# A hybrid decoder layer: the sparse-attention indexer and half of its top-k search interleaved with a reordered input projection, fp32 products in place of hi/lo stacks

## What is computed

```python
s = jnp.einsum('bqhd,bsd->bqhs', qi, ki).astype(jnp.float32)          # 8 indexer heads of 64
score = jnp.einsum('bqhs,bqh->bqs', jax.nn.relu(s), wi) * IDX_SCALE
score = jnp.where(causal[None], score, -jnp.inf)
_, sel = lax.top_k(score, n_sel)                                      # 256 keys of each query
k_sel = gather(k, sel); v_sel = gather(v, sel)
logits = jnp.einsum('bqhd,bqkd->bhqk', q, k_sel) * DSA_HD ** -0.5     # 4 heads, one key head
a = jax.nn.softmax(logits, axis=-1)
return jnp.einsum('bhqk,bqkd->bqhd', a, v_sel)
```

## Time and profile before

| | |
|---|---|
| median of 3 runs | 2062.38 us (2059.34 to 2068.35) |
| span of the profiled execution | 2056.5 us |
| TensorE busy | 1782.8 us (87%), weight loads 1599.2 us |
| DVE busy | 1014.8 us (49%) |
| ACT busy | 629.8 us (31%) |
| POOL busy | 39.9 us (2%) |
| projection | 37 to 297 us |
| values, maps, index stage | 297 to 417 us |
| diff and sdiff items | 417 to about 760 us |
| dsa and sdsa items | about 760 to 947 us |
| output projection, MLP, embedding, last norm | 947 us to the end |

### The profile page before, as it was taken

One profiled execution on the slowest core, in us unless ns is written; L12 is line 12 of the kernel. 1 busy time (PEld: TensorE's weight loads), 2 busy tenths in 40 slices (PEclk: granted clock), 3 DMA queues, 4 the chain that ended last, 5 costly groups with the idle time before them and its releaser, 6 DMA issues.

```text
span 2056.5 us, 26558 instructions
## 1 busy us (share of the span) xinstructions
PE 1782.8 (87%) x9933; PEld 1599.2 (78%) x9933; DVE 1014.8 (49%) x2033; ACT 629.8 (31%) x1083; POOL 39.9 (2%) x43
## 2 busy tenths in 40 slices
PE   3999996847788976998979999999999999998794
PEld 3999983424455665667969999999899899998794
DVE  5113406787778885333344444534443443454643
ACT  3111125555456733443122211121121121113321
POOL 0000000000000002001000000000000000000000
PEclk9999996855566555887989999999999999999897
DMA  3111112111211112113101111111111111120102
GB/s 143 41 51 41 51 53 61 27 41 57 67 42 41 42 41 62 31 32 142 45 27 42 41 52 42 42 42 45 49 41 42 42 42 51 41 67 31 31 31 84
DMA packets 48043, 102.80 MB, mean 50 GB/s; under 512 B 5378, under 2 KB 21762, under 8 KB 47938
## 3 DMA queue, kind: packets, MB, share of 16 engines
q1 hardware_dynamic: 45506, 92.44, 14.4%
q0 software_dynamic: 2432, 8.92, 1.2%
HBM read 93.69 MB, written 7.66 MB: 49 GB/s over the span
## 4 chain that ended last, share of the span: by engine, by line
PE 68%; DVE 13%; issue 9%; ACT 4%; SPq 2%; DMA 2%; POOL 1%; DVEq 0%; POOLq 0%; ACTq 0%
PE ps L213 41%; PE ps L1364 10%; PE ps L533 3%; PE ps L494 2%; PE ps L519 2%; DVE TN L818 2%; PE ps L447 1%; DVE TN L266 1%; DVE Z L971 1%; PE ps L1499 1%; SPq L1101 1%; PE ps L545 1%; PE ps L1185 1%; DMA pages<-in_d_pages 1%; SPq L1102 1%
## 5 line engine op out<-in xcount | busy, mean ns | idle before, releaser
L213 PE MATMUL ps<-xh,wh 128*128 128x352 f32 x1968 | 640.7, 326 | 34.6 <-DVE xl L271 21.6
L213 PE MATMUL ps<-xh,wl 128*128 128x352 f32 x1968 | 638.0, 324 | 0.0
L213 PE MATMUL ps<-xl,wh 128*128 128x352 f32 x1968 | 637.7, 324 | 0.0
L213 PEld LDWEIGHTS ps<-xh,wh 128*128 128x128 f32 x1968 | 372.7, 189 | 40.5 <-issue 26.2
L213 PEld LDWEIGHTS ps<-xh,wl 128*128 128x128 f32 x1968 | 372.7, 189 | 0.0
L213 PEld LDWEIGHTS ps<-xl,wh 128*128 128x128 f32 x1968 | 372.3, 189 | 0.0
L204 ACT ACTIVATE wh<-wr 128x1024 fp32r<-128x1024 f32 x106 | 112.1, 1059 | 849.6 <-PE ps L213 604.8
L208 DVE TENSOR_TENSOR wl<-wr,wh 128x1024 fp32r<-128x1024 f32 x106 | 129.5, 1223 | 431.2 <-ACT wh L204 431.1
L1364 PE MATMUL ps<-ah,wh 128*128 128x352 f32 x528 | 175.3, 332 | 18.0 <-DVE Z L1443 17.9
L1443 DVE TENSOR_TENSOR Z<-Z,ps 128x352 f32<-128x352 f32 x264 | 134.5, 520 | 98.3 <-PE ps L1364 97.8
L1364 PE MATMUL ps<-al,wh 128*128 128x352 f32 x528 | 169.9, 322 | 0.0
(11 more groups left out here) (247 smaller groups left out, 1884.7 us busy)
## 6 DMA issues: line engine op xcount, KB each, us to landing
wr<-in_weights SPq DMA_DIRECT2D x106, 512.0 KB, 3.6
pages<-in_d_pages SPq DMA_DIRECT2D x64, 256.0 KB, 2.9
pages<-in_c_pages SPq DMA_DIRECT2D x64, 96.0 KB, 1.9
Z<-in_xT SPq DMA_DIRECT2D x8, 528.0 KB, 8.7
Z<-in_xT POOLq DMA_DIRECT2D x8, 528.0 KB, 8.1
out_y<-TN SPq DMA_DIRECT2D x8, 528.0 KB, 2.7
arena<-in_c_pages SPq DMA_DIRECT2D x64, 64.0 KB, 1.8
out_d_k<-Z POOLq DMA_DIRECT2D x2, 528.0 KB, 6.5
```

Of the source, the lines that this page charges most:

```text
L213: last = nc.tensor.matmul(out, w_at(w), x_at(x), start=start and t == 0, stop=stop and t == 2)
```

## The change

- **Order of the blocks.** `IN_COLS` begins with the keys (sparse keys with indexer keys, then values with the indexer's head weights), then four blocks of indexer queries (2 to 5), then D's six, then A (12 to 17), B (18, 19) and the sparse queries (20, 21). The loops over blocks are written out. Block n uses banks 0 to 2, whatever n; ACT copies it chunk by chunk, and block n's chunk c waits for the copy of chunk c of block n-1. Block 0 is copied twice, so that keys lie on both halves of the partitions.
- **Index units.** 40 units in place of 48 steps: a tile's keys in pieces of 512 columns, by pairs of heads. A unit is two fp32 products of 64 rows, straight from `Z`, into banks 3, 4 or 5, 6; one Relu over both; two multiply-adds. Unit u sits in block 6 + u // 9, after the third, the sixth or the last piece of the contraction. The samples' products run together at the end of block 10, their scores in block 11; their pages are loaded one sample a block in blocks 2 to 9.
- **Search.** Signs in blocks 6, 7, 10 and 11; the 15 high steps in blocks 12 to 21, at chunks 1 and 2 but where a convolution or a pooling sits. Halves are no longer copied apart: `y_hi` and `y_lo` are 16-bit views with a step of two of the fp32 magnitudes. In the items: ties 1 to 3, low steps 4 to 19, masks 20 to 26.
- **dsa items.** Logits are fp32 products of 64 rows from `Z`; `kstack`, `dq_stack` and the copies and casts that filled them are gone.
- **Placement.** Scores and magnitudes lie in `Z`, constants in three loads, values in `dtok` (256 columns) and `ctok`; POOL stores keys and values during the projection.

```diff
+IN_COLS = ([[(1280, 64), (1928, 64)], [(1344, 64), (1920, 8)]]
            + [[(1408 + 128 * j, 128)] for j in range(4)]
+           + [[(2248, 128)], [(2376, 128)], [(1992, 128)], [(2120, 128)], [(2504, 128)], [(2632, 128)]]
+           + [[(a + 128 * j, 128)] for j in range(2) for a in (256, 512, 0)]
+           + [[(768, 128)], [(896, 128)], [(1024, 128)], [(1152, 128)]])
...
+        UNITS = [(i, a, min(512, (i + 1) * P - a), p) for i in TILES for a in range(0, (i + 1) * P, 512) for p in range(4)]
+        IDX_BLOCK = 6
+        def unit_at(n, c, stage):
+            u = 9 * (n - IDX_BLOCK) + 3 * c + stage - 1
+            return u if 0 <= u < NU else None
...
-        def pe_idx(pe):
-            for u, (i, h) in enumerate(IDX):
-                if u >= 2:
-                    pe.wait_ge(idx_relu, u - 1)
...
-                    for t, q in enumerate((wh, wl)):
-                        last = nc.tensor.matmul(flat(u % 2)[:, a:a + w], q[:, i % 2, h], kstack[:, a:a + w], start=t == 0, stop=t == 1)
...
+        def pe_idx_unit(pe, u):
+            i, a, w, p = UNITS[u]
...
+            if u >= 2:
+                pe.wait_ge(idx_relu, u - 1)
+            for h in range(2):
+                r = slice(HD * h, HD * h + HD)
+                last = nc.tensor.matmul(bank(3 + 2 * (u % 2) + h)[:, 0:w], Z[r, QI + p, i * P:(i + 1) * P], Z[r, KI2, a:a + w],
+                                        start=True, stop=True)
+            last.then_inc(idx_mm, 1)
...
+                for c in range(3):
+                    pe.wait_ge(evac, 3 * n + c - 2)
+                    for k in range(KC):
+                        last = three_pass(bank(c)[:, 0:TC], lambda w: w[:, n % 2, k], lambda x: x[:, k, c * TC:(c + 1) * TC],
+                                          k == 0, k == KC - 1)
+                        if k == KC - 1:
+                            last.then_inc(w_used if c == 2 else proj_mm, 1)
+                        if k in (2, 5, 7):
+                            pe_fill(pe, n, c, (2, 5, 7).index(k))
...
+        def act_project(act):
+            for n in range(NZ):
+                for c in range(3):
+                    for stage in range(2):
+                        u = unit_at(n, c, stage)
+                        if u is not None:
+                            act_idx_unit(act, u)
+                    if (n, c) in STEP_AT:
+                        act_counts(act, STEP_AT[n, c], act_junk_p)
+                    act_evacuate(act, n, c)
+                    if c == 2 and n + 2 < NZ:
+                        split_hi(act, n + 2, n % 2, n // 2 + 2)
...
-        HI_BITS = range(2, 17)
-        TIES = {17: range(0, 3), 18: range(3, 5), 19: range(5, NTOP)}
-        LO_BITS = range(20, 36)
-        MASKS = {36: NTOP - 1} | {37 + j: j for j in range(NTOP - 1)}
+        PLACES = [(n, c) for n in range(N_G, NZ) for c in (1, 2) if c == 2 or (n, 0) not in (*CONV_AT, *POOL_AT)]
+        STEP_AT = {place: k for k, place in enumerate(PLACES[:HI_STEPS])}
+        TIES = {1: range(0, 3), 2: range(3, 5), 3: range(5, NTOP)}
+        LO_ITEMS = range(4, 4 + LO_STEPS)
+        MASKS = {20: NTOP - 1} | {21 + j: j for j in range(NTOP - 1)}
...
+                    else:
+                        part, q, k = slice(HD * (h % 2), HD * (h % 2) + HD), CQ[h // 2], KC2
                     for a in range(0, S, 512):
                         w = min(512, S - a)
-                        if kind == "dsa":
-                            for t in range(2):
-                                last = nc.tensor.matmul(out[:, a:a + w], dq_stack[:, (tile_no(n) - QT) % 2, t, h], kstack[:, a:a + w],
-                                                        start=t == 0, stop=t == 1)
-                            continue
...
+        def pe_sidx(pe):
+            pe.wait_ge(k_in, 16 * NPG * DB)
+            pe.wait_ge(copied, 1)
+            pe.wait_ge(idx_relu, NU)
+            pe.wait_ge(wsel_set, 2)
             for j, (a, w) in enumerate(COLS):
+                for b in range(DB):
+                    half = slice(HD * (b % 2), HD * (b % 2) + HD)
...
+            sp.wait_ge(pt_in, 16)
+            for n in range(2, NZ):
+                sp.wait_ge(w_lo, n - 1)
+                sp.dma_start(wr[:, n % 2], d["weights"][n]).then_inc(w_raw[n % 2], 16)
+                if n < 2 + DB:
+                    sp_idx_pages(sp, n - 2)
+            sp.wait_ge(w_used, NZ)
+            sp.dma_start(late, d["late"]).then_inc(s_late, 16)
             sp_diff_pages(sp)
             sp_dsa_pages(sp)
```

More of the change, by code:

```diff
@@ new lines, in act_ctok, with act_idx_unit @@
+        def act_ctok(act):
+            for b in range(3):
+                act.wait_ge(c_tr, b + 1)
+                rows, m = (P, 4) if b < 2 else (NS, 1)
+                src = bank(7 - b)[0:rows, 0:m * P].rearrange("p (t f) -> p t f", f=P)[:, :, 0:72]
+                nc.scalar.activation(ctok[0:rows, 4 * b:4 * b + m], src, ACT.Copy).then_inc(c_cp, 1)
+        def act_idx_unit(act, u):
+            i, a, w, p = UNITS[u]
+            act.wait_ge(idx_mm, u + 1)
+            if u >= 2:
+                act.wait_ge(idx_acc, u - 1)
+            b = 3 + 2 * (u % 2)
+            nc.scalar.activation(relu[:, u % 2, :, 0:w], ps8[:, b:b + 2, 0:w], ACT.Relu, scale=IDX_SCALE).then_inc(idx_relu, 1)
@@ L684, in act_item @@
                         half = slice(HD * (h % 2), HD * (h % 2) + HD)
-                        last = nc.scalar.activation(samples(Z[half, GH + h // 2])[:, 2 * i:2 * i + 2], o[:, h], ACT.Copy)
+                        last = nc.scalar.activation(samples(YC[half, h // 2])[:, 2 * i:2 * i + 2], o[:, h], ACT.Copy)
                 last.then_inc(so_cp, 1)
@@ L813, in col, with scores_of @@
             return tk[0:rows, a] if j is None else tk[0:rows, a, j:j + 1]
+        def scores_of(src, j, rows=None):
+            at, S, full = scores(j)
+            r = slice(0, full if rows is None else rows)
+            return SC[r, at:at + S] if src is SC else src(r, at, S)
         def count(j, src, scalar, op, out):
@@ new lines, in sidx_out @@
+        def sidx_out(g, j, rows, w):
+            return bank(3 + 2 * g + j)[rows, 0:w] if j < 2 else bank(7)[rows, 64 * g:64 * g + w]
+        def pe_sidx(pe):
[3 more added lines that the diff above has]
+            pe.wait_ge(wsel_set, 2)
+            for j, (a, w) in enumerate(COLS):
+                for b in range(DB):
+                    half = slice(HD * (b % 2), HD * (b % 2) + HD)
+                    keys = kring[b // 2][half].rearrange("p g c -> p (g c)")[:, a:a + w] if j < 2 else Z[half, KI2, SEQ:NT]
+                    r = 32 * (b % 4)
+                    last = nc.tensor.matmul(sidx_out(b // 4, j, slice(r, r + 32), w), qis[half, b // 2].rearrange("p h t -> p (h t)"),
+                                            keys, start=True, stop=True)
@@ L1194, in pe_sscore, with act_sidx @@
             last.then_inc(sscore_mm, 1)
-        def act_sidx(act, g):
-            act.wait_ge(sidx_mm, 4 * g + 4)
-            for j, (a, w) in enumerate(COLS):
-                last = nc.scalar.activation(srelu[:, g, a:a + w], bank(4 + j)[:, 0:w], ACT.Relu, scale=IDX_SCALE)
-            last.then_inc(sidx_relu, 1)
+        def act_sidx(act):
+            act.wait_ge(sidx_mm, 1)
+            act.wait_ge(idx_acc, NU)
+            for g in range(2):
+                for j, (a, w) in enumerate(COLS):
+                    last = nc.scalar.activation(srelu[:, g, a:a + w], sidx_out(g, j, slice(0, P), w), ACT.Relu, scale=IDX_SCALE)
+                last.then_inc(sidx_relu, 1)
```

699 lines of the change are left out of this document (341 added, 358 removed).

## The result

| | before | after |
|---|---|---|
| median | 2060.86 us (2052.95 to 2068.35, 8 runs) | 2073.16 us (2071.79 to 2077.17, 8 runs) |
| ratio to before | | 1.0066, 95% interval 1.0049 to 1.0083 |
| span of the profiled execution | 2056.5 us | 2071.9 us |
| TensorE busy | 1782.8 us | 1845.2 us |
| mean granted clock | 0.873 | 0.855 |

The change makes the kernel 0.7% slower. The forecast was 2011.5 us; what happened is the third rival, whose price was 2077 us.

What follows compares the result with a forecast made beforehand. TensorE bounds the projection, a ring the stretch behind it; diff tiles were read singly. Terms: -40 (up to item 0), -23 (items), +12 (dsa items) = -51 us, giving 2011.5 us; forecast 1995 to 2030 (chance 0.50), overall range 1980 to 2056.

Steps and rivals of the forecast that it cites:

- the third rival: dsa items: 64-row fp32 products lower the clock; at 0.55 the stage takes 66 us more, kernel 2077 us; chance 0.08.
- the price of the dsa items: dsa items: 14 us more full-speed work, at clock 0.81 a stage of 149 us, 12 us more.
- the second rival: Tiles 5 to 7: TensorE idles less, clock rises from 0.61 to 0.8, 30 us less, kernel 1981 us; chance 0.14.
- step a: Projection, from block 6: 40 index units, halves side by side, 28 us, plus 10 us for row-layout changes and semaphore waits.
- step (b): Projection: 16 sample products in sequence, 15 us with the short ones; scores 3.7 us; transposes and small products 2 us.
- (c): Projection: TensorE's waits for bank copies, Relus and a late DVE, 3 us of stalls; bounds 0 and 15.
- (d): Projection, blocks 12 to 21: 15 high search steps cost TensorE nothing; if cover failed, up to 3 us a block.
- the ring: sdiff items: page load, logits, three items and values in turn take 40 us a tile; tiles 1 to 3 unchanged.
- Rivals 1: Projection inserts cost more: halves in sequence (28 us), stalls reach 10; kernel 2046 us; chance 0.20.
- 4: Page ring holds all tiles and DVE's work delays splits, giving back most of the 40 us; kernel 2055 us; chance 0.08.
- the 40 us: Up to item 0: 104 us saved behind the projection, net of 64 us added to it.

Runs made afterwards that it cites:

- the last experiment: Block 20's third-chunk copy put ahead of the three Signs on ACT, against the 128-row fp32 kernel with three half-buffers for sdiff pages (1980.9 us): 1975.12 us.

## Why the prediction was wrong

**The step that failed is the price of the dsa items.** The work in it was right: 14 us more at full clock forecast, 11 measured. (Its 14 us count all columns of the tiles from 2 on, and some of the first tile's are issued ahead of the stretch.) The work was multiplied by the clock of the kernel before, 0.81, as though the clock were a property of the stage. It followed what TensorE executes: 0.81 with fp32 logits of 128 rows, 0.52 with 64, in the same stage. The prediction named this sign itself: a dsa clock under 0.6 would make it wrong. The forecast for items 47 to 75 was 132.1 + 12 = 144 us; they took 215.2. That is 71 us, and the whole miss of the median is 62 (2073.2 against 2011.5).

**How the rival was weighed.** Case 3 had the mechanism and nearly the time, and got 0.08. That its 2077 is only 4 us off is in part luck: the stage grew by 83 us where it had 78, and what stands ahead of it became 69 us shorter where it had 63. Against it stood the slices 16 and 17 at 0.8, which held three sample items with 64-row logits. But those are 15.2 us in a stage of 132 (L504 above), and the edit adds 46 at the lower clock, or 28 at the higher. For it stood the diff tiles, busy 93% and held at 0.62, with logits of 32 rows. That row was the nearest to the case, because it alone had TensorE full and few rows at once. I used it for the second rival as well, and there to say that the clock would not rise. A row that is used against a gain in one place counts for the loss in the other.

**The projection: right in sum, with errors that cancel.** It took 324 us, as forecast. The units ran side by side; one of 512 columns with the block's products around it, and the sample products:

```profile
126.34 0.32 PE L240 MATMUL ps<-xl,wh 128*128 128x352 f32 x1
126.59 1.13 PE L478 MATMUL ps<-Z 64*128 64x512 f32 x4
127.65 0.43 PE L240 MATMUL ps<-xh,wh 128*128 128x352 f32 x1
127.92 0.32 PE L240 MATMUL ps<-xh,wl 128*128 128x352 f32 x1
...
216.81 3.76 PE L1265 MATMUL ps<-Z,TN 64*32 64x512 f32 x48
```

From the product ahead of the unit to the second behind it are 1.58 us, where two steady distances of 0.16 are 0.32: the unit costs 1.26 us. Forecast was 0.86 + 0.25 = 1.11 (step a), and the 40 units together were 44 us (the 96 us of the first window below, less 324 block products at 0.16) where 38 were forecast: the changes of the row layout were booked too low. The last row is step (b): the sixteen sample products took 3.8 us with the short ones, not 15, since they ran four at a time on average. Steps (c) and (d) failed the other way. TensorE did not idle at all while the units ran (117 to 213 us), nor in the steps of the search up to 340 us, as two windows show:

```profile
117.00:213.00 96.00, 96.00 (x484) 62.75 (x483) 59.07 (x105) 46.95 (x70) 1.10 (x2) 1.00 0.13 42
...
233.00:340.00 107.00, 107.00 (x669) 106.91 (x668) 86.76 (x222) 63.54 (x114) 0.53 (x1) 1.00 0.12 40
```

So the 3 us for stalls were not needed; but the high steps, booked at nothing, cost some 9 us in the last block. Eleven and 3 us too many, 6 and 9 too few: the 324 us came out by luck. The text named the cover ("each has most of a block") and the price without it, but not the place: block 20 holds a pooling of 11 us and a step, and ACT's Signs wait for both. As the last experiment shows, this stall was hardly on the path to the items either (1.2 us), since what starts them is the end of the search's last step and the last copy behind it. Item 0 began at 375.6, where 376 was forecast.

**The items: the parts right, one size off.** Tiles 1 to 3 took 41.0 to 42.1 us, held by the ring, as read. Tile 0 took 26.4 us, 7.8 less than before (forecast 7 less). Tile 4 was to take 2.5 us more than its 42.5 and took 8.6 more: its masks hold it, but DVE was booked at 41 us and was busy 44.7 of the 51.1. Tiles 5 to 7 took 43.5, 41.2 and 38.9 us, below the 45 forecast, and gave back more than tile 4 took. The total, 27.8 us less against 23, held.

**Rivals 1, 2 and 4 did not occur.** The inserts ran side by side; the clock in tiles 5 to 7 rose only from about 0.61 to 0.60, 0.67 and 0.65; the 40 us stood.

## What to carry to other kernels

Where TensorE is nearly always busy, price a stage as its full-speed work divided by its clock, and treat the clock as something that the change can move. Here products of 64 rows in place of 128 took it from 0.82 to 0.52, and 260 value products beside them from a mean of 308 to 419 ns. Filling the other half of the rows with the same operands at half size, or with zeros, brought the clock back to 0.81 at no more full-speed work on TensorE (108 against 109 us). When the rate of a stage is carried over to a changed stage, look for the row that is most like the stage after, not the one that is nearest in time.

## What was not expected of the hardware

- **Rows and the clock.** The same stage, TensorE busy 91 to 97% of it: 0.52 with 64-row logits, 0.81 with 128 rows, 0.81 with 128 rows of which half multiply by zero, 0.68 with two 64-row products side by side. The Trainium skill (TensorE: Matmul & The Clock Gate, "What's actually happening") ties the granted clock to how busy the engine has been. This case's trace differs: at 97% busy it held 0.52. The same page (Why this matters for your kernels) says that a single product of 32 rows takes as long as one of 128; for 64 rows, at one clock, this case agrees (109 us of full-speed work in the stage with 64 rows, 108 with 128), but the rule says nothing of the clock.
- **Row tiles and a bank.** The sample products of samples 0 to 3 lie on both halves of the rows and share a bank, and those of 4 to 7 another; all ran four at a time on average (48 instructions in 3.76 us, where the long ones one behind the other would be 13.8 us by the 0.86 of the earlier trace rows). The prediction drew on the rule of the Trainium skill (TensorEngine Tiling (Array Packing), Gotcha 1) that two row tiles can't access one bank at the same time. By it I took 13.8 us for the long ones; the measurement decides, and they cost about a quarter of that.
- **Equal instructions, unequal clock.** In the versions with fp32 logits of 128 rows the dsa stage took 133.7 us at 0.87 in two profiles and 137.8 to 143.0 at 0.80 to 0.83 in five. What tips it is open: the instructions are the same, the kernels differ ahead of the stage, each has one profile, and no run took it apart.
